# Other distances in memory between the activations and the ring of weights, chosen for each stage

## What is computed

```python
for l in range(DEPTH):                                  # 2
    h = rms_norm(x, norm1_g[l])
    z = h @ w_in[l]
    ...
    merged = (g[:, :, 0] * (o_a @ w_br_mla[l])
              + g[:, :, 1] * (o_b @ w_br_gla[l])
              + g[:, :, 2] * (o_c @ w_br_s5[l]))
    x = x + merged @ w_out[l]
    h2 = rms_norm(x, norm2_g[l])
    x = x + jnp.square(jax.nn.relu(h2 @ w_ff1[l])) @ w_ff2[l]
# second block
h = rms_norm_2(x, g_pre_mix[l])
z = h @ w_in[l]
...
merged = jax.nn.sigmoid(z_ga) * y_attn + jax.nn.sigmoid(z_gc) * y_conv
x = x + rms_norm_2(merged @ w_mix_out[l], g_post_mix[l])
h = rms_norm_2(x, g_pre_ffn[l])
x = x + rms_norm_2(swiglu_ffn(h, w_ffn_in[l], w_ffn_out[l]), g_post_ffn[l])
```

## Time and profile before

| | |
|---|---|
| runs | 1487.55, 1487.82, 1490.46 us |
| median | 1487.82 us |
| profiled execution, its own time | 1488.56 us |
| its span, first to last instruction | 1486.8 us |
| TensorE busy | 1447.3 us (97%) |
| granted clock, mean over the span | 0.997 |
| weight slabs split by POOL | 154 and 206 of 2.4 us each |

### The profile page before, as it was taken

One profiled execution on the slowest core, in us unless ns is written; L12 is line 12 of the kernel. 1 busy time (PEld: TensorE's weight loads), 2 busy tenths in 40 slices (PEclk: granted clock), 3 DMA queues, 4 the chain that ended last, 5 costly groups with the idle time before them and its releaser, 6 DMA issues.

```text
span 1486.8 us, 24141 instructions
## 1 busy us (share of the span) xinstructions
PE 1447.3 (97%) x9839; PEld 1293.7 (87%) x9839; DVE 754.2 (51%) x1419; ACT 697.7 (47%) x1020; POOL 862.4 (58%) x364
## 2 busy tenths in 40 slices
PE   7999999999999999999999999999999999899998
PEld 7976778989999897677898889989999988799997
DVE  4978867521112697886742221229994454321112
ACT  5644225545444564422554534455445655643444
POOL 5710000878888671000087888878885536688886
PEclk9999999999999999999999999999999999999999
DMA  6632344556666563333455667656664433466664
GB/s 194 178 103 72 98 114 128 188 172 195 187 193 189 159 177 89 85 99 100 141 191 178 194 207 241 191 156 189 194 186 127 134 108 116 140 184 187 196 185 142
DMA packets 321555, 234.48 MB, mean 158 GB/s; under 512 B 9446, under 2 KB 304901, under 8 KB 321444
## 3 DMA queue, kind: packets, MB, share of 16 engines
q1 hardware_dynamic: 321444, 232.93, 53.2%
HBM read 231.82 MB, written 1.09 MB: 157 GB/s over the span
## 4 chain that ended last, share of the span: by engine, by line
PE 83%; issue 5%; ACT 4%; POOL 3%; DVE 3%; DMA 1%; SPq 0%; DVEq 0%; POOLq 0%; ACTq 0%
PE ps L726 19%; PE ps L2049 13%; PE ps L2029 6%; PE ps L2030 6%; PE ps L2031 6%; PE ps L1112 6%; PE ps L1113 6%; PE ps L1114 6%; POOL w_lo L1340 3%; DMA raw<-in_w_in_dram 1%; PE ps L1187 1%; PE ps L2169 1%; PE ps L2183 1%; PE ps L2150 1%; PE ps L1224 1%
## 5 line engine op out<-in xcount | busy, mean ns | idle before, releaser
L1340 POOL TENSOR_TENSOR w_lo<-raw,w_hi 128x1024 fp32r<-128x1024 f32 (+1 forms) x206 | 491.4, 2402 | 478.5 <-ACT w_hi L1374 477.9
L794 POOL TENSOR_TENSOR w_lo<-raw,w_hi 128x1024 fp32r<-128x1024 f32 x154 | 370.8, 2418 | 135.5 <-ACT w_hi L816 135.1
L1374 ACT ACTIVATE w_hi<-raw 128x1024 fp32r<-128x1024 f32 (+1 forms) x206 | 217.0, 1057 | 212.2 <-PE ps L726 90.8
L1112 PE MATMUL ps<-h_hi,w_hi 128*128 128x256 f32 x864 | 243.8, 282 | 1.7 <-POOL w_lo L794 1.0
L1113 PE MATMUL ps<-h_lo,w_hi 128*128 128x256 f32 x864 | 241.4, 279 | 0.0
L1114 PE MATMUL ps<-h_hi,w_lo 128*128 128x256 f32 x864 | 241.4, 279 | 0.0
L2029 PE MATMUL ps<-h_hi,w_hi 128*128 128x256 f32 (+1 forms) x816 | 230.4, 282 | 5.4 <-DVE h_lo L1648 3.3
L2030 PE MATMUL ps<-h_lo,w_hi 128*128 128x256 f32 (+1 forms) x816 | 228.4, 280 | 0.0
L2031 PE MATMUL ps<-h_hi,w_lo 128*128 128x256 f32 (+1 forms) x816 | 228.3, 280 | 0.0
L816 ACT ACTIVATE w_hi<-raw 128x1024 fp32r<-128x1024 f32 x154 | 161.9, 1058 | 139.0 <-PE ps L1114 61.3
L2049 PE MATMUL ps<-hN,raw 128*128 128x256 f32 x768 | 174.9, 383 | 0.0
(11 more groups left out here) (340 smaller groups left out, 2442.1 us busy)
## 6 DMA issues: line engine op xcount, KB each, us to landing
raw<-in_w_in_dram SPq DMA_DIRECT2D x160, 512.0 KB, 3.8
raw<-in_w_ff_dram SPq DMA_DIRECT2D x128, 512.0 KB, 4.0
raw<-in_w_ffn_in_dram SPq DMA_DIRECT2D x44, 512.0 KB, 3.8
raw<-in_w_ffn_out_dram SPq DMA_DIRECT2D x22, 512.0 KB, 3.3
raw<-in_w_out_dram SPq DMA_DIRECT2D x16, 512.0 KB, 3.2
raw<-in_w_br_gla_dram SPq DMA_DIRECT2D x8, 512.0 KB, 3.4
raw<-in_w_br_mla_dram SPq DMA_DIRECT2D x8, 512.0 KB, 4.0
raw<-in_w_br_s_dram SPq DMA_DIRECT2D x8, 512.0 KB, 3.4
```

The lines of the kernel that those rows point to most:

```text
L794: nc.gpsimd.tensor_tensor(out=w_lo[(NS * L + i) % RING][:, 0:kt * n], in0=raw[(NS * L + i) % RING][:, 0:kt * n], in1=w_hi[(NS * L + i) % R ...
L1112: MM(out, w[0], x[0], start=first_k, stop=False, skip_group_check=skip)
L1340: nc.gpsimd.tensor_tensor(out=w_lo[(NS * l + i) % RING][:, 0:kt * n], in0=raw[(NS * l + i) % RING][:, 0:kt * n], in1=w_hi[(NS * l + i) % R ...
L1374: A_(w_hi[(NS * l + i) % RING][:, 0:kt * n], raw[(NS * l + i) % RING][:, 0:kt * n], ACT.Copy)\
```

## The change

h_hi and h_lo become views into one tensor HR, which is 64 elements longer than the two and their filler were (W_OFF is 80 in place of 16). The function h_parts(stage) returns the two views, 8192 bytes apart, at a place such that from each view to the ring it is APART[stage] bytes modulo 512: norm 1 of the two layers 128 and 192, output projections 0, norm 2 of the two layers 256 and 320, second block's first norm 160, its convolution 96, its FFN 224. Whoever writes or reads the views of a stage takes the same ones. No instruction is added, removed or moved on any engine, and no wait.

The ring and everything allocated behind it lie 256 bytes further than before: w_hi at 49600. xt and hN, allocated ahead of it, stay, so hN to raw is 0 modulo 512 in place of 256; the differences among the others stay as they were.

```diff
@@ -224,7 +224,9 @@
     HALF_IN = {0: 5, 2: 6, 4: 7}
     NU = U_FF + NCH
     PG_BANKS = 3
-    W_OFF = 16
+    W_OFF = 80
+    APART = {"norm1_0": 128, "norm1_1": 192, "merged": 0, "norm2_0": 256, "norm2_1": 320,
+             "mix": 160, "conv": 96, "ffn": 224}
     PGF = 2
 
     ctx = ExitStack()
@@ -244,9 +246,12 @@
         mid = ExitStack()
         MD = sb("MD", [P, 10240 + W_OFF], c=mid)
         mid.close()
-        h_hi = sb("h_hi", [P, KD, T], f32r)
-        h_lo = sb("h_lo", [P, KD, T], f32r)
-        sb("w_off", [P, W_OFF])
+        HR = sb("HR", [P, 2 * KD * T + W_OFF], f32r)
+
+        def h_parts(stage):
+            at = W_OFF - APART[stage] // 4
+            return [HR[:, at + KD * T * i:at + KD * T * i + KD * T].rearrange("p (k t) -> p k t", k=KD) for i in range(2)]
+
         w_hi = [sb(f"w_hi{i}", [P, SLAB], f32r) for i in range(RING)]
         w_lo = [sb(f"w_lo{i}", [P, SLAB], f32r) for i in range(RING)]
         sq = sb("sq", [P, KD, T])
@@ -660,7 +665,9 @@
                 if j % 2:
                     ins.then_inc(hf_ok.s, 1)
 
-        def norm_lo(dve, stt, l, gain_col, gain, at=0):
+        def norm_lo(dve, stt, l, gain_col, gain, h, at=0):
+
+            h_hi, h_lo = h
@@ -732,6 +743,8 @@
 
         def projection(pe, MM, l, weights):
 
+            h_hi, h_lo = h_parts("merged")
+
             for k in range(KD - 2):
                 w = weights(k)
                 if k % 2 == 0:
@@ -933,7 +947,7 @@
-                        A_(piece(h_hi, p), piece(CA, p), ACT.Copy).then_inc(ch_ok.s, 1)
+                        A_(piece(h_parts("conv")[0], p), piece(CA, p), ACT.Copy).then_inc(ch_ok.s, 1)
@@ -1090,7 +1105,7 @@
-            norm_lo(dve, stt, L, col2, "g_pre_ffn", NP)
+            norm_lo(dve, stt, L, col2, "g_pre_ffn", h_parts("ffn"), NP)
@@ -1159,7 +1174,7 @@
-                    last = product(J0 + t, pair(u % 3)[:, t % 2, :], 0, h_hi, h_lo,
+                    last = product(J0 + t, pair(u % 3)[:, t % 2, :], 0, *h_parts("conv" if J0 == J_CO else "mix"),
@@ -1244,7 +1259,7 @@
-                        product(up2_at(c) + 2 * s + m, pair(u % 3)[:, m, :], 0, h_hi, h_lo,
+                        product(up2_at(c) + 2 * s + m, pair(u % 3)[:, m, :], 0, *h_parts("ffn"),
@@ -1385,6 +1400,7 @@
+                    h_hi, h_lo = h_parts(f"norm{k + 1}_{l}")
@@ -1674,7 +1690,7 @@
-                norm_lo(dve, stt, l, col, "norm1_g")
+                norm_lo(dve, stt, l, col, "norm1_g", h_parts(f"norm1_{l}"))
@@ -1986,7 +2002,7 @@
-                norm_lo(dve, stt, l, col, "norm2_g", NP)
+                norm_lo(dve, stt, l, col, "norm2_g", h_parts(f"norm2_{l}"), NP)
@@ -2067,7 +2083,7 @@
-
+                h_hi, h_lo = h_parts(f"norm1_{l}")
@@ -2112,7 +2128,7 @@
-                    product(l, i, out, 0, n, h_hi, h_lo, fresh=None if t else 0).then_inc(used.s, 1)
+                    product(l, i, out, 0, n, *h_parts(f"norm1_{l}"), fresh=None if t else 0).then_inc(used.s, 1)
@@ -2404,7 +2420,7 @@
-                        product(l, i, pair((U_FF + c) % PGF)[:, m, :], 0, P, h_hi, h_lo,
+                        product(l, i, pair((U_FF + c) % PGF)[:, m, :], 0, P, *h_parts(f"norm2_{l}"),
```

More of the change, by code:

```diff
@@ L836, in h_rounded @@
             def h_rounded(k, gain, upto):
+                h_hi, h_lo = h_parts(("mix", "ffn")[k])
                 prep(upto)
@@ L994, in dve_second @@
             dve.wait_ge(cols2_ok.s, 4)
-            norm_lo(dve, stt, L, col2, "g_pre_mix")
+            norm_lo(dve, stt, L, col2, "g_pre_mix", h_parts("mix"))
             link(V.memset(Up[:, :, 0:CONVW - 1], 0.0))
@@ L1082, in dve_second @@
                         dve.wait_ge(ch_ok.s, p + 1)
-                        tt(piece(h_lo, p), piece(CA, p), piece(h_hi, p), ALU.subtract).then_inc(cl_ok.s, 1)
+                        c_hi_, c_lo_ = h_parts("conv")
+                        tt(piece(c_lo_, p), piece(CA, p), piece(c_hi_, p), ALU.subtract).then_inc(cl_ok.s, 1)
             pair_lo(3)
@@ L1138, in token_major @@
             def token_major(out, w, half):
+                h_hi, h_lo = h_parts("mix")
                 for b in range(NT):
```

## The result

The kernel after takes 1496.3 us (median of four, 1495.13 to 1497.92), the kernel before beside it 1488.88 (1487.55 to 1490.46): ratio 1.005, 95% interval 1.0033 to 1.0068. The prediction was 1481, range 1471 to 1491.5, so both the sign and the range were wrong. The profiled execution has a span of 1496.1 us against 1486.8, +9.3.

A forecast was written before the change was run, and what follows sets the result against it. TensorE, busy 97%, was taken to bound the kernel. Slow products -6.8, fast ones turning slow +0.5 and projections -0.7 gave -7.0 us: 1488.56 to 1481.6, less 0.74 for the median, 1481 us; range 1471 to 1491.5.

The forecast's parts named there:

- TensorE bounds it, and the rate of the starts is what can change: Whole kernel: TensorE busy 1447.3 of 1486.8 us, so only how long each matmul holds it can move the end.
- Two rates at 64 bytes in the kernel before: Products on h: starts 113.4 or 117.8 ns apart at the same 64 bytes, 4.4 ns per matmul between them.
- Part 1: Output projections, 64 to 0 bytes: 288 matmuls at 227 instead of 229 ns, -0.7 us.
- the mixed stages: z, glu, q, k, gates and conv output: 2640 matmuls, some 1150 of them slow, forecast to stay as they are, 0.
- a draw: Products on h: stream and weight load fall into one of a few locks, drawn again at each interruption; -6.8 and +0.5 us.
- the third, 120 ns: Products on h: upper bound per matmul from the u and o2 rows; all 5520 there cost +19 us, 1507; chance 0.03.
- my own sign of being wrong: Listed as wrong: a third rate in a stage of thousands, idle time before L1113 or L2030, or rates without order by distance.
- Modulo 512: Distances between h and the ring: counted as repeating every 512 bytes, so 256 and 320 were priced as new distances.
- Rival E: Products on h: if what repeats is not 512 bytes, distances mean something else, a draw or nothing; no separate chance given.
- Rival D: Products on h: 64 bytes is the best distance, others slower; sum +3.5 us, 1491; chance 0.17.
- Part 3: Beside the products on h: ring and what follows lie 256 bytes further, hN against raw from 256 to 0; 0 us.
- Rival C: Products on h: place has no say, the moment alone decides, same locks return; -2 to +2 us, 1486 to 1490; chance 0.25.

The follow-up runs named there:

- 64: The changed kernel with all eight distances at 64 bytes, ring still 256 bytes further: 1486.51 us against 1487.38 for the kernel before, ratio 0.9999.
- 144: The changed kernel with 144 bytes in all stages of h, output projections 0: 1479.65 us, ratio 0.9951 to the kernel before.
- 256: The changed kernel with 256 bytes in all stages of h, output projections 0: 1503.83 us, ratio 1.0112 to the kernel before.
- the map: Probe with nothing else running, not a changed kernel: 256 chains, 16 ring places by 16 distances modulo 256 in steps of 16 bytes; 1719.6 us.

## Why the prediction was wrong, point by point

- *TensorE bounds it, and the rate of the starts is what can change*: right. The time before, after and in the experiments follows that rate; TensorE's idle time inside a stage changes by 1.2 us at most between the traces of before, after, 64, 144 and 256.
- *Two rates at 64 bytes in the kernel before*: right as read, and the map shows the same two at 64: 113.3 and 117.8 ns.
- *Part 1, the projections, -0.7 us*: right; 2.72 us for twelve starts as forecast, -0.5 in the traces.
- **The step that failed: "the mixed stages ... are my sample of a draw: four in ten slow. With that share everywhere ..."** It took the two rates of one distance for two locks that every distance shares. The runs show that each distance has rates of its own. 64 with the ring at a multiple of 32 is one that can go two ways; 128, 160, 192, 224 and 0 never reached 113.3 there. The slow stages were ones that a new draw "can hardly harm" only within the two rates seen; the third, 120 ns, stood in my own rows for u and o2, where I used it as a bound and gave it 0.03; a third rate in a stage of thousands was also my own sign of being wrong, and it came. Forecast -6.8 + 0.5; measured by stage, in the order of the table, +0.4, +2.4, +0.7, -0.1, +6.3 and -1.0 us, together +8.7.
- *Modulo 512*: the unit was taken from the change. It is 256, so 256 and 320 bytes were no new distances but 0 and 64. Rival E named this and was priced as a draw. With the right unit, u at 0 in the earlier trace rows was a direct forecast for the first FFN at 256: 120 against the measured 119.8. And y at 224 in the earlier trace rows, 118.7 and 116.5, had the second FFN's 116.7 between its two values.
- *Rival D, slower*: the right mechanism and sign, and its size came from reading between three distances as if the rate changed smoothly. It put the mixed stages at +1.8 us; they took +6.3, since 160 bytes is one of the worst distances (120.0) and 96 lies at 117.4. FFN of the first block +1.5 forecast, +2.3 measured; second FFN -0.2 and -1.0. The z's +1.1 were met in length by luck: their rates rose by 3.6 and 1.4 ns, which is 2.7 us for twice 552 matmuls, and shorter waits and the slow first matmuls of before hide the rest. With 113.3 ns at 144 and 120.0 at 160, no two rows can be read between.
- *Part 3, nothing beside it*: right, though 0 and 256 turned out to be the same distance modulo 256. 383 ns at both, no idle time inside a stage that grew, and the kernel at 64 in all stages stands within 0.2% of the one before.
- *Rival C, place has no say*, and with it what the Trainium skill says (SBUF — State Buffer, Who interferes with whom): fell. One probe with TensorE alone has 113.3 to 123.3 ns for one instruction shape by the place of its two operands. The page's rule that TensorE waits on no one is about other engines, and those were idle; that its own two reads are independent of each other is not what these rows suggest, since the rate goes by where the two operands lie to each other. That it is the reads that meet isn't shown.
- *The gap that the Trainium skill gives* (TensorE: Matmul & The Clock Gate, Back-to-back issue gap), by which I estimated 109 ns: that section gives it for an isolated matmul, and says that in a stream of loads and matmuls both set the spacing. The trace doesn't reach 109: no chain of this three-pass kind, at any place, was under 113.3.

What stays open: why 113.3 is the floor, what repeats every 256 bytes of distance and every 32 of place, whether a matmul meets its own weights' load or the next one's (the chains meant for it let the place change too), and what sends a chain at 64 to the one rate or the other.

## What to carry to other kernels

Where TensorE is busy all the time, read the distance between starts by stage before anything else; one shape at several rates with no wait is a sign that the place of its operands counts. Then measure a map of place and distance in a probe of one engine (a few us a point) instead of choosing distances one by one in the kernel, keep the absolute place in it as a second axis, and give each form of the product its own entry: what is best where the activations stream (144, or 64 with the ring 16 bytes off) is not best for 512 columns of weights (0, ring at a multiple of 32). And when a trace shows two values at one setting, don't take them for the values of every setting.

## What the runs showed of the hardware

- Chains of float32r products of 256 columns, three passes, start 113.3 to 123.3 ns apart with nothing else at work; no chain's steady mean is under 113.3, and 226.7 for 512 columns is twice that.
- The rate follows the distance between the streamed operand and the weights modulo 256, to 4 bytes (144: 113.3; 140: 121.9; 148: 120.0), and the place modulo 32: 27 us of 1480 for a shift of 16 bytes that keeps the distances between h and the ring (4 of them in the downs, 1 in the projections).
- With h_hi and w_hi at the good distance, h_lo or w_lo elsewhere is enough for 115.6 to 120.3 ns.
- Plain float32 products of the same shape take 383 ns each and start 215.9 ns apart at 0, 224 and 256 bytes (modulo 256 two distances), all alike.
